# Two halves of the tokens at every norm, and the last down projection split the same way

## What is computed

```python
for layer in range(2):
    hn = rms_norm(h, norm_mix_g[layer])
    h = h + hybrid_mixer(hn, ...)          # attention heads and a gated convolution, then @ w_out
    hn = rms_norm(h, norm_ffn_g[layer])
    g, u = split(hn @ w_up)                # 2816 columns each
    h = h + (silu(causal_dwconv(g)) * u) @ w_down
return rms_norm(h, final_g)
```

## Time and profile before

| what | us |
|---|---|
| median of 3 runs (2687.03 to 2687.76) | 2687.05 |
| the profiled execution, its own time | 2686.18 |
| its span from first to last instruction | 2684.4 |
| PE busy | 2532.3 |
| DVE busy | 1604.8 |
| POOL busy | 816.5 |
| ACT busy | 624.5 |

### The profile page before, as it was taken

One profiled execution on the slowest core, in us unless ns is written; L12 is line 12 of the kernel. 1 busy time (PEld: TensorE's weight loads), 2 busy tenths in 40 slices (PEclk: granted clock), 3 DMA queues, 4 the chain that ended last, 5 costly groups with the idle time before them and its releaser, 6 DMA issues.

```text
span 2684.4 us, 29574 instructions
## 1 busy us (share of the span) xinstructions
PE 2532.3 (94%) x12006; PEld 2103.9 (78%) x12006; DVE 1604.8 (60%) x1979; ACT 624.5 (23%) x1161; POOL 816.5 (30%) x437
## 2 busy tenths in 40 slices
PE   6999998899999999999889999979999999999994
PEld 4888886777888888888678888868788888888883
DVE  6555677535566665566674467763465555666555
ACT  3344443321011010000214434443210001001002
POOL 4221213142333333333432111222433333333332
PEclk9999999899999999999999999979999999999996
DMA  3100001211111111111210000121111111111111
GB/s 129 32 24 32 24 32 40 74 48 40 47 48 48 48 55 47 47 48 47 102 40 24 32 24 32 32 79 39 40 44 55 48 47 48 48 51 52 48 40 63
DMA packets 50583, 127.32 MB, mean 47 GB/s; under 512 B 4496, under 2 KB 22032, under 8 KB 50448
## 3 DMA queue, kind: packets, MB, share of 16 engines
q1 hardware_dynamic: 47856, 120.05, 13.8%
q10 hardware_dynamic: 2592, 5.38, 0.5%
HBM read 116.76 MB, written 8.39 MB: 47 GB/s over the span
## 4 chain that ended last, share of the span: by engine, by line
PE 82%; DVE 13%; ACT 3%; issue 2%; POOL 0%; DMA 0%; DVEq 0%; ACTq 0%; POOLq 0%
PE ps L416 24%; PE ps L418 24%; PE ps L417 23%; PE ps L530 3%; DVE x_lo L857 3%; PE ps L517 2%; DVE h L903 2%; PE ps L490 1%; PE ps L504 1%; ACT prob L740 1%; PE ps L505 1%; DVE h L901 1%; DVE prob L937 1%; PE ps L457 1%; DVE q_next L904 1%
## 5 line engine op out<-in xcount | busy, mean ns | idle before, releaser
L416 PE MATMUL ps<-x_hi,w_hi 128*128 128x512 f32 x2304 | 908.9, 394 | 13.4 <-POOLq L345 8.9
L418 PE MATMUL ps<-x_hi,w_lo 128*128 128x512 f32 x2304 | 899.5, 390 | 0.0
L417 PE MATMUL ps<-x_lo,w_hi 128*128 128x512 f32 x2304 | 898.4, 390 | 0.0
L340 POOL CAST w_hi<-stage 128x1024 fp32r<-128x1024 f32 (+1 forms) x198 | 207.2, 1047 | 1751.2 <-PE ps L418 1662.6
L342 POOL TENSOR_TENSOR w_lo<-stage,w_hi 128x1024 fp32r<-128x1024 f32 (+1 forms) x198 | 522.4, 2639 | 15.9
L416 PEld LDWEIGHTS ps<-x_hi,w_hi 128*128 128x128 f32 x2304 | 433.8, 188 | 106.3 <-POOLq L345 13.1
L418 PEld LDWEIGHTS ps<-x_hi,w_lo 128*128 128x128 f32 x2304 | 433.4, 188 | 92.0
L417 PEld LDWEIGHTS ps<-x_lo,w_hi 128*128 128x128 f32 x2304 | 434.2, 188 | 87.5
L862 DVE TENSOR_TENSOR h<-ps,h 128x1024 f32<-128x1024 f32 x352 | 431.1, 1225 | 79.3 <-PE ps L418 39.5
L416 PE MATMUL ps<-q_split,w_hi 128*128 128x512 f32 x704 | 277.1, 394 | 10.7 <-DVE q_split L1105 10.7
L417 PE MATMUL ps<-q_split,w_hi 128*128 128x512 f32 x704 | 275.7, 392 | 0.0
(11 more groups left out here) (132 smaller groups left out, 2267.5 us busy)
## 6 DMA issues: line engine op xcount, KB each, us to landing
stage<-stream SPq DMA_DIRECT2D x180, 512.0 KB, 3.3
stage<-stream SPq DMA_DIRECT2D x16, 448.0 KB, 4.6
h<-x_t ACTq DMA_DIRECT2D x8, 512.0 KB, 9.4
h<-x_t SPq DMA_DIRECT2D x8, 512.0 KB, 3.3
saved_h<-h SPq DMA_DIRECT2D x8, 512.0 KB, 3.0
h<-saved_h SPq DMA_DIRECT2D x8, 512.0 KB, 3.4
out_t<-h SPq DMA_DIRECT2D x8, 512.0 KB, 3.0
stage<-stream SPq DMA_DIRECT2D x16, 64.0 KB, 4.9
```

The source lines that it names most:

```text
L340: pool.tensor_copy(w_hi[:, s, wide], stage[:, s, wide]).then_inc(pool_seq, 1)
L416: pe.matmul(out, w_hi[:, s, w], hi, start=start, stop=False)
L417: pe.matmul(out, w_hi[:, s, w], lo, start=False, stop=False)
L418: return pe.matmul(out, w_lo[:, s, w], hi, start=False, stop=stop)
```

## The change

- Every norm is done in two halves of the tokens. ACT, DVE and POOL instructions on 1024 tokens become two on 512. `start_normed` does everything of half 0 first and then half 1; `spread(0)` stands inside half 1, and `spread(1)` in the middle of the next projection (`project(spreading=True)`).
- The last down projection of a layer (`last_down`) goes by halves: 8 feature tiles of half 0, then 8 of half 1, through four single banks, with adds of 512 tokens.
- For the last feature tile DVE makes the gated product ahead of the adds of the tile before. For this `mix_hi` and `mix_lo` are double-buffered (`q_split` and `k_twice` in turn).
- Behind the norm of the feed-forward part DVE takes the halves of gate and up in another order.
- In the last norm ACT makes no `x_hi`. POOL does three of the eight output tiles, DVE five. Output and input move in 16 DMAs of 256 KB.
- The reciprocal root keeps `y` in PSUM.
- `weight_plan` changes only the count of the last down tile: the two tiles behind a norm still wait for four halves.

```diff
             def sums_and_splits():
                 split()
-                start_sums()
+                start_sums(0)
                 split()
-                end_sums()
+                end_sums(0)
+                start_sums(1)
+                end_sums(1)
...
+            def last_down(layer):
+                s = ready(next_tile())
+                pe.wait_ge(mix_ready, seen(mix_ready))
+                for n in range(2 * KT):
+                    t, m = n // KT, n % KT
+
+                    pe.wait_ge(add_done, half_added(layer, 0, 0) - 1 + max(0, n - len(LAST_DOWN) + 1))
+                    three_pass(bank(LAST_DOWN[n % len(LAST_DOWN)]), s, slice(m * P, (m + 1) * P),
+                               mix_hi[LAST][:, halves_of_t[t]], mix_lo[LAST][:, halves_of_t[t]], True, True)\
+                        .then_inc(down_done, 1)
+                down_tiles[0] += 2 * KT
...
             def start_normed(order):
                 tiles = (next_tile(), next_tile())
-                banks = (PROJ, SPARE)
                 for t in range(2):
                     take_bank(PROJ + t)
-                for n, first_bank in zip(tiles, banks):
-                    s = ready(n)
-                    for k in order:
-                        w = slice(k * P, (k + 1) * P)
-                        if n == tiles[0]:
-                            pe.wait_ge(x_hi_ready, seen(x_hi_ready))
-                        for t in range(2):
+                    for n, first_bank in zip(tiles, (PROJ, SPARE)):
+                        s = ready(n)
+                        for k in order:
+                            w = slice(k * P, (k + 1) * P)
+                            if n == tiles[0]:
+                                pe.wait_ge(x_hi_ready, seen(x_hi_ready))
                             pe.matmul(bank(first_bank + t), w_hi[:, s, w], x_hi[:, k, halves_of_t[t]],
                                       start=k == order[0], stop=False)
                             pe.matmul(bank(first_bank + t), w_lo[:, s, w], x_hi[:, k, halves_of_t[t]],
                                       start=False, stop=False)
-                sum_squares()
-                for n, first_bank in zip(tiles, banks):
-                    for k in order:
-                        w = slice(k * P, (k + 1) * P)
-                        if n == tiles[0]:
-                            pe.wait_ge(x_lo_ready, seen(x_lo_ready))
-                        for t in range(2):
+                        if t and n == tiles[0]:
+                            spread(0)
+                    for n, first_bank in zip(tiles, (PROJ, SPARE)):
+                        for k in order:
+                            w = slice(k * P, (k + 1) * P)
+                            if n == tiles[0]:
+                                pe.wait_ge(x_lo_ready, seen(x_lo_ready))
                             ended = pe.matmul(bank(first_bank + t), w_hi[:, n % W_SLOTS, w],
                                               x_lo[:, k, halves_of_t[t]], start=False, stop=k == order[-1])
-                            if k == order[-1]:
-                                half_ends(first_bank + t, ended)
-                spread()
+                        half_ends(first_bank + t, ended)
+                        if n == tiles[0]:
+                            sum_squares(t)
...
+            def start_norm(order, g_of):
+                absorb(0, order, g_of)
+                partial(0)
+                absorb(1, order, g_of)
+                dve.wait_ge(eye_in, 16)
+                roots(0)
+                partial(1)
+                dve.wait_ge(rstd_ready, seen(rstd_ready))
+
+            def end_norm():
+                roots(1)
                 dve.wait_ge(rstd_ready, seen(rstd_ready))
...
+                else:
+                    value()
+                    for m in range(KT):
+                        if m == 2:
+                            value_rest(f)
+                        add_down(m)
...
+            for t in range(2):
+                partial(t)
+                roots(t)
+            for t in range(2):
+                dve.wait_ge(rstd_ready, seen(rstd_ready))
+                for m in OUT_BY_DVE:
+                    dve.scalar_tensor_tensor(h[:, m, halves_of_t[t]], h[:, m, halves_of_t[t]],
+                                             gain_of(DEPTH - 1, V_NEXT_G, m), rstd_all[:, halves_of_t[t]],
+                                             ALU.mult, ALU.mult).then_inc(out_ready, 1)
```

More of the change, by code:

```diff
@@ L185, in build @@
         ps = ctx.enter_context(nc.psum_tensor("ps", [P, 8, HALF], f32))
-        mix_hi, mix_lo = q_split[:, 0, :], q_split[:, 1, :]
+        mix_hi, mix_lo = ([m[:, n, :] for m in (q_split, k_twice)] for n in range(2))
         shuffled, gated_x, gated_b = h[:, 5, :], h[:, 4, :], h[:, 5, :]
@@ L387, in _ @@
                     split()
-            start_sums()
-            end_sums()
+            for t in range(2):
+                start_sums(t)
+                end_sums(t)
+            pool.wait_ge(out_scaled, len(OUT_BY_POOL))
+            for t in range(2):
+                pool.wait_ge(rstd_ready, 4 * DEPTH + t + 1)
+                for m in OUT_BY_POOL:
+                    part = h[:, m, halves_of_t[t]]
+                    pool.tensor_tensor(part, part, rstd_all[:, halves_of_t[t]], ALU.mult).then_inc(out_by_pool, 1)
         @block.tensor
@@ L455, in sum_squares @@
+            def sum_squares(t):
                 pe.wait_ge(partial_ready, seen(partial_ready))
-                for b in range(QB):
-                    ended = pe.matmul(ps[:, HEAD, b:b + 1], squares[0][:, b * P:(b + 1) * P], ones[:, 0:1],
+                for b in range(QB // 2):
+                    block_of_t = slice(t * HALF + b * P, t * HALF + (b + 1) * P)
+                    ended = pe.matmul(ps[:, SUMS[t], b:b + 1], squares[0][:, block_of_t], ones[:, 0:1],
                                       start=True, stop=True)
@@ L459, in sum_squares, with spread @@
                 ended.then_inc(sum_done, 1)
-            def spread():
+            def spread(t):
                 pe.wait_ge(diag_ready, seen(diag_ready))
-                for t in range(2):
-                    ended = pe.matmul(bank(SCORE + t), ones[:, :], diagonal[:, halves_of_t[t]], start=True, stop=True)
-                ended.then_inc(spread_done, 1)
+                pe.matmul(bank(SCORE + t), ones[:, :], diagonal[:, halves_of_t[t]], start=True, stop=True)\
+                  .then_inc(spread_done, 1)
@@ L637, in _ @@
                 start_normed(OUT_ORDER)
+                project(spreading=True)
                 project()
-                project()
-                down()
-                for _ in range(F_TILES - 2):
+                down(0)
+                for f in range(1, F_TILES - 1):
                     project()
                     project()
-                    down()
-                down(pairs=2)
-            sum_squares()
-            spread()
+                    down(f)
+                last_down(layer)
+            for t in range(2):
+                sum_squares(t)
+                spread(t)
         @block.scalar
@@ new lines, in prepare_ffn @@
+                for t in range(2):
+                    act.wait_ge(half_done, done + 2 * KT - 1 + t)
+                    for m in OUT_ORDER[:-1]:
+                        head_tile(m, t, gain_of(layer, V_FFN_G, m))
+                    act.wait_ge(evac_done, done + 2 * KT - 1 + t)
+                    head_tile(last, t, gain_of(layer, V_FFN_G, last))
+                    square_tile(KT - 1, last, t)
+            def prepare_next(layer):
+                for t in range(2):
+                    for m in range(KT):
+                        act.wait_ge(add_done, half_added(layer, m, t))
+                        square_tile(m, m, t)
+                        if layer < DEPTH - 1:
+                            head_tile(m, t, gain_of(layer, V_NEXT_G, m))
@@ L833, in _ @@
                 prepare_next(layer)
-            keep_rstd()
+            for t in range(2):
+                act.wait_ge(squares_ready[t], KT * (2 * DEPTH + 1))
+            for m in OUT_BY_POOL:
+                act.activation(h[:, m, :], h[:, m, :], ACT.Copy, scale=gain_of(DEPTH - 1, V_NEXT_G, m))\
+                   .then_inc(out_scaled, 1)
+            keep_rstd(0)
+            keep_rstd(1)
         @block.vector
@@ L1080, in out_projection, with convolve_gates @@
                         add_out(layer, m, t, PROJ + t)
-            def hidden(layer, f):
-                for t in range(2):
-                    evacuate(t, padded[:, TAPS - 1:], PROJ + t)
+            def convolve_gates(layer, f):
                 dve.wait_ge(evac_done, half[0])
```

238 lines of the change are left out of this document (139 added, 99 removed).

## The result

The changed kernel takes **2700.64 us** (median of 5 runs, 2699.32 to 2702.31) against 2687.35 of the kernel before in the same rounds (2687.03 to 2687.76): a ratio of 1.0052, 95% interval 1.0040 to 1.0063. It is 13.3 us slower. The forecast was 2685.0, with a range of 2668 to 2700.

A forecast was written before the change was run, and what follows sets the result against it. PE was taken as the bound, with gains or losses only at norms, last down projections and both ends. End -13.4, start -3.4, middle -0.4, feed-forward norms +15.2 give -2.0 us off the 2687.05 median: 2685.0, range 2668 to 2700.

The forecast's parts named there:

- step 5: Feed-forward norm: PE waits 3.6 us for POOL's third-tile split, then 12 matmuls take 2.7; half 1's rstd at 637.0.
- Step 4: Feed-forward norm: the low clock ahead of the passes' end keeps costing 2.8 us; passes end at 629.2, before 624.4.
- third rival: Behind each norm: PE's clock falls once more, 3.6 us more at four norms, 2699; chance 0.22.
- step 6: Feed-forward norm to second projection: DVE takes 10.0 us instead of 12.2; PE resumes at 647.8 instead of 640.16.
- Step 2: Feed-forward norm: DVE's half x_lo take turns with POOL's split and seven half adds; half 0's partial sums end at 609.7.
- the turns cost nothing: Rival at the norms: engines find gaps between shorter instructions, 31 us won in all, 2656; chance 0.17.
- PE keeps its full clock: Rival at the norms: more evenly spread work keeps the clock up, 3.2 us off three norms, 2675; chance 0.13.
- ACT starts at 15.1: Start: sixteen input issues delay ACT from 14.4 to 15.1, but its first instruction is x_hi of half 0.
- the chain is then ACT, x_lo to 34.9, root to 38.0: Start: these steps, then matmuls, spread and a sum, end the passes at 47.5, before 54.7; 3.4 us won.
- if spread(0) waits for DVE: Sign of a wrong forecast: the root's place behind both absorb costs more than the forecast gives it.
- 7.2 us won there: Last down projection of layer 0: starts at 1317.0, takes 10.9 us at full clock, ends at 1327.9 instead of 1335.2.
- The end: End of the kernel: first output DMA at 2656.9 instead of 2671.39, span end 2671.0; 13.4 us won, range 10 to 16.

The follow-up runs named there:

- e2: The changed kernel with four unused matmuls filling PE's wait for the third weight tile's split behind each inner norm: 2692.21 us.
- e1: The changed kernel with the third weight tile behind each inner norm split after three halves instead of four: 2680.39 us, ratio 0.9976.
- b4: b3 with the iterated value of the last two roots in PSUM and the changed kernel's order of operations: 2663.72 us, ratio 0.9913.
- b2: b1 with POOL splitting the third weight tile behind a norm after two halves of four: 2671.99 us, ratio 0.9943.
- e3: The changed kernel with POOL's first three adds for half 1 ahead of the second weight tile's split in the feed-forward norms: 2693.3 us.
- s2: The changed kernel with POOL's second split in layer 0 behind the rotary angle, and the input as eight whole transfers: 2696.79 us.
- r1: s2 with DVE making the root of half 0 ahead of the x_lo of half 1 in all norms: 2694.24 us.
- c2: The changed kernel with e1, e3 and s2 together, and the root of half 0 ahead of half 1's x_lo: 2672.26 us, ratio 0.9943.
- b1: The kernel before with only the last gated product ahead of the adds, mix_hi and mix_lo double-buffered: 2673.27 us, ratio 0.9950.
- b3: b2 with layer 1's last down projection and final norm by halves, the root's small values in SBUF: 2666.72 us, ratio 0.9922.

## Why the prediction was wrong

The sum was -2.0 us and the span came out +14.0. Of the 16.0 us between, the start holds 9.4 and the two feed-forward norms 8.1 (3.5 and 4.6); the end gives 1.4 back and the middle 0.2.

**The failed step of the norms is step 5**, "now PE waits the whole split, 1.04 + 2.35 and hand-over, 3.6 us. Then 12 matmuls (2.7)". The wait is right to 0.1 us (3.69). The matmuls behind it run at half clock and take 5.4. Step 4 had counted the low clock only where the earlier trace rows already showed it, ahead of the passes' end. That a new wait of this length would bring a second one was my third rival, at 0.22, "it decides if the granted clock reads 0.50 right behind the wait": it does, at 637 to 643. e2 shows it alone, with the wait filled and nothing else: 8.4 us. The rival's 14 us were not its price, though: part of it lies behind step 6's wait (3.22 us, clock 0.50 at 657 to 659), which step 6 had forecast as about 3 us, without a term for its clock, and which neither e1 nor e2 takes away. The kernel before waits 1.99 and 0.83 us at these two places, with the granted clock at 1.00 behind both; 3.69 and 3.22 bring a drop, and so does 3.2 in e1, at 646 to 648. The length of the wait doesn't decide it alone. In b4, at the same place and with the same code as in b2, a wait of 1.93 us was followed by the low clock, and its 12 matmuls took 4.4 us:

```profile
626.04 0.47 PE L440 MATMUL ps<-x_hi,w_hi 128*128 128x512 f32 x1 [1.93 <-DVE padded L912]
...
627.00:629.00 2.00, 2.00 (x6) 1.55 (x5) 1.24 (x1) 1.98 (x2) 0.00 (x0) 0.50 0.71 262
```

What decides it there is open. The case to which I had given 0.22 came true in its mechanism. That its 2699 lies so near 2700.6 is luck: it put 14 us on the four norms, and 9.4 of the 16.0 us lie in the start, for most of which it had no term.

**The other steps of the norm held.** Step 2's turns of half size put the sum at 609.7, measured 608.8 on the same footing. The `x_lo` of half 1 took 5.4 us where 4.9 were forecast, which cost nothing, and the passes were over at 628.2 (629.2). e3 took three turns out of each feed-forward norm and won 7.3 us where its expectation had 7.6; only 2.4 to 2.5 us a norm came from the turns, where 3.8 were expected, and the rest from the shorter stretch at the low clock, so the agreement in size is partly luck. So the rival "the turns cost nothing" falls, and with the clock at 0.50 the rival "PE keeps its full clock" too.

**The start failed in three terms.** "ACT starts at 15.1": it was 17.3. The change puts POOL's second split ahead of the sums, where it meets DVE's angle, and one instruction of 0.23 us took 2.39 and another 0.99. I had counted every instruction that the change adds, but not what the moved one meets. s2, which undoes that meeting and the sixteen issues, brings the first x_hi to 14.4. Second, "the chain is then ACT, x_lo to 34.9, root to 38.0": x_lo ended at 41.8 and the root at 44.8, for DVE's eight x_lo of half 1 took 8.3 us and stood in front of the root; that is the doubt I had named ("if spread(0) waits for DVE"), and r1 and c2 remove it. Third, the low clock. It comes behind the 3.69 us at 59.5, as in the other norms, and also earlier, behind the first small sum: step 4 had counted that stretch in the feed-forward norm, and the sum for the start had no such term. r1 shows it. There the root of half 0 is no longer in the way and `spread(0)` follows at 42.8, near the forecast, and yet the passes end at 52.1 instead of 47.5, with PE at the low clock from 34 to 41:

```profile
36.00:38.00 2.00, 2.00 (x7) 1.52 (x6) 1.82 (x7) 0.00 (x0) 0.00 (x0) 0.50 0.01 4
```

How the terms share the 9.4 us is open: s2 wins 1.8 us of the start as its attention begins, r1 still loses 3.6 by its seam, and c2, the only run that is ahead there, doesn't wait the 3.69 us either.

**The end of layer 0 held.** "7.2 us won there": b1, which has that part alone, wins 7.1, and b2, b3 and b4, which have it too, win 6.1. With the halved norm behind it the net is -0.6, forecast -0.4, but in that norm two errors cancel. Less the 17.1 us by which it begins late, the passes are over at 1363.0 (forecast 1365.2). Then the matmuls behind the wait of 3.69 us run at a clock of 0.50, and `rstd` of half 1 is there at 1372.8 (1373.0).

**The end won 14.8 instead of 13.4.** b1 wins 5.9 of it by the earlier product alone, and b4 8.4 more by halves: there nothing of the next tile is queued behind the halves, and the stores begin under the second root.

So the change holds two good parts, the product first and the halves at the end, and one bad one, the halves in front of a projection. b4 keeps the first two and the earlier split: 23.5 us less than the kernel before. Even c2, with most of the losses mended that I found, stays 8.5 us behind it.

## What to carry to other kernels

Where two engines take turns by the instruction, count the other engine's instructions that will stand beside yours, and their length. Half an instruction takes half a turn, but here seven half adds stood where two whole ones had, and the eight `x_lo` won 2.3 us of 16.1. Look also at what a moved instruction meets at its new place. A wait of PE is priced with the matmuls behind it: in the earlier trace rows a wait of 2.0 us cost 2.0, and in the changed kernel one of 3.7 cost 6.3 (2.6 more for 12 matmuls). But in b4 one of 1.93 brought the low clock too, so read the granted clock behind each wait. And a wait in a trace names only its latest cause; before removing it, look for the next one in line.

## What the hardware showed that I had not expected

- One operand in PSUM keeps a small DVE instruction out of the turns with POOL: 1.18 us and 0.16 us for the same operation on 128x4 (b3, b4). The Trainium skill, "SBUF — State Buffer", section on the two separate sides, names as takers of the lock DVE instructions with two SBUF inputs and those in a two-port mode; the slow SCALAR_TENSOR_TENSOR has both its inputs in SBUF, and there the trace agrees. Whether the slow TENSOR_SCALAR, with one source, ran in a two-port mode no trace here shows.
- ACT's sixteen issues of half transfers took 8.89 us, the eight whole ones 4.66, and 5.03 to 5.32 in c2, r1 and s2: an issue took 0.56 us at 256 KB and 0.58 to 0.67 at 512 KB, so halving the bytes made it hardly cheaper.
